# Low parts of the branch stage's weight slabs in pieces of 256 columns instead of 512

## The chip, the cores and the metric

The kernel runs on one core of one Trainium2 chip. The metric is the device time of one execution in microseconds, as the median of several runs; a profiled execution stands beside them.

## The reference

One layer of a transformer followed by the first layer of another, on 512 tokens of 1024 features, all in fp32:

```python
h = h + 0.5 * swiglu(rms_norm(h, ffn1_norm[i]), ...)          # up1, down1
u = rms_norm(h, mix_norm[i])
z = u @ w_in[i]                                               # the branch stage ("mix") begins
(aq, ak, av, iq, ik, iw, rq, rk, rv, rg, ga, gb) = jnp.split(z, split_points, axis=-1)
...
y_a = dsa_attention(aq, ak, av, iq, ik, iw, n_sel)            # top-k attention on roped aq, ak, iq, ik
y_r = group_norm_heads(retention(rq, rk, rv), ret_gn[i]) * jax.nn.silu(rg)
merged = jax.nn.sigmoid(ga) * (y_a @ w_branch_a[i]) + jax.nn.sigmoid(gb) * (y_r @ w_branch_b[i])
h = h + merged @ w_out[i]                                     # the branch stage ends
h = h + 0.5 * swiglu(rms_norm(h, ffn2_norm[i]), ...)          # up2, down2
gate = jax.nn.sigmoid(rms_norm(h, ple_norm[i]) @ w_ple_gate[i])
h = h + gate * (p[i] @ w_ple_proj[i])                         # ple
```

Then a gated linear attention mixer and a feed-forward block with a short convolution (gla, up3, down3), and a last norm. The stage that the change touches is the one from the product with `w_in` to the product with `w_out`.

## The kernel before

Activations lie feature-major: 8 chunks of 128 features by 512 tokens. A weight matrix is read as slabs of 128 partitions by up to 1024 columns (`SLAB = 8 * P`), one slab for each tile of 128 output features. Every product is made three times for fp32 accuracy: a weight and an activation are each split into a high part (`w_hi`, `u_hi`, in the rounded type fp32r) and a low part, the remainder (`w_lo`, `u_lo`). TensorE multiplies low by high, high by low and high by high into one accumulator (L1592 to L1594, 24 matmuls of 512 columns for a tile; L1782 to L1784 for the tiles of `rva`, with 328 columns).

A slab passes through a ring of `RING = 4` slots. SyncE loads it into `w_raw`; ScalarE copies it to `w_hi` in one instruction (L660, `hi_ready`); GpSimd subtracts, `w_lo = w_raw - w_hi` (`lo_part`, L574 to L579), and its last instruction counts up `lo_ready`. That semaphore tells TensorE that the slab can be used, and SyncE that the slot of `w_raw` can be loaded again. ScalarE may overwrite `w_hi` of a slot once TensorE has finished the tile that used it. So the low part of a slab is made some tiles ahead of its use.

The order of the branch stage is written out by hand in the list `MIX` (L76). Each engine walks through it and does its share of every step. A step such as `("rq", 0)` is a tile of a projection, `("to", k, ...)` stands for the part of a tile's contraction up to chunk k, between which small steps (index scores, retention scores, logits, attention) are placed. On GpSimd (L618 to L637) the loop before each step makes the low parts of the slabs up to four slots ahead of the step, then the step's own work: `rotate` for the ROPE steps (L608, L610, L612: a product with the cosine, one of the swapped halves with the sine, their sum, 512 columns each), the addition of the negative mean to `rv` (L629), and the low part of the retention output (L635). All of that stands in one queue, in the order of `MIX`.

Two accumulations of the program matter around it. The accumulator has `BANKS = 4` banks in PSUM, and tile t needs tile t - 4 to have been read out (`tile_freed`). The ROPE tiles are read out by VectorE (L1248) into one of two buffers of `gate_t`, so VectorE waits before the z-th of them until GpSimd has finished the rotation two before (`rope_ready`, L1246). The halves are swapped by DMAs that SyncE issues (L526), in one queue with the slab loads (L470) and the copies of the rotated keys (L530, L531), which wait for the first rotation.

The first steps of the stage, in the order of PSUM tiles: rg (head 0, half 0), kk, iq 0 to 3, rq 0, rk 0, rg (head 0, half 1), then the four tiles of `rva` (v of head 0, av and iw, token-major, one tile for 128 tokens). Their matmuls go chunk by chunk over all four tiles, so the four banks must be free within the first chunk:

```python
for c in range(first, upto):
    ...
    for tt in range(NT):
        if c == 0:
            free_bank(t + tt)
```

Of the kernel before, what the change touches and what calls it, by code (L numbers as in the profile page):

```python
# [45 lines left out]
RING = 4  # L46
# [3 lines left out]
SLAB = 8 * P  # L50
# [134 lines left out]
def layer_program(nc, A, out):  # L185
    plan = Plan()
# [11 lines left out]
    with ExitStack() as ctx:  # L198
# [221 lines left out]
        def nth(steps, step):  # L420
            return steps.index(step)
# [146 lines left out]
        @block.gpsimd  # L568
        def _(pool):
            pool.memset(ones[:, :], 1.0).then_inc(consts_set, 1)  # L570
            pool.memset(eps[:, 0:1], NORM_EPS).then_inc(consts_set, 1)
            pool.memset(eps[:, 1:2], GN_EPS).then_inc(consts_set, 1)

            def lo_part(slot, width, count):  # L574
                pool.wait_ge(hi_ready, count)
                for at in range(0, width, SLAB // 2):
                    part = slice(at, min(at + SLAB // 2, width))
                    ins = pool.tensor_tensor(w_lo[:, slot, part], w_raw[:, slot, part], w_hi[:, slot, part].bitcast(F32), ALU.subtract)  # L578
                ins.then_inc(lo_ready, 1)  # L579

            def lo_run(n0, n1):

                rounds = (n1 - n0) // RING
                if rounds:
                    with pool.Fori(0, rounds) as i:
                        for j in range(RING):
                            lo_part((n0 + j) % RING, SLAB, i * RING + (n0 + j + 1))
                for n in range(n0 + rounds * RING, n1):
                    lo_part(n % RING, SLAB, n + 1)

            def lo_down(n0):
                with pool.Fori(0, 2) as i:
                    for j in range(4 * DOWN_SLABS):
                        lo_part((n0 + j) % RING, plan.width[n0 + j], i * (4 * DOWN_SLABS) + (n0 + j + 1))

            def rotate(of):

                kind, z = of[0], nth(rope_steps, of)
                cos, sin = (cos_r[:, :], sin_r[:, :]) if kind in ("rq", "rk") else (cos_a, sin_a)
                dst = {"kk": lambda: wts[:, 0:S], "iq": lambda: q8[:, of[1], :], "aq": lambda: q8[:, of[1], :],  # L600
                       "rq": lambda: rqk[:, 0, :], "rk": lambda: rqk[:, 1, :]}[kind]()
                x, y = gate_t[:, z % 2, :], up_t[:, z % 2, :]
                pool.wait_ge(tile_freed, plan.first[of][1] + 1)
                if kind in ("rq", "rk") and of[1]:
                    pool.wait_ge(rs_done, NT * of[1])
                if kind == "aq":
                    pool.wait_ge(idx_scored, A_HEADS * len(index_units))
                pool.tensor_tensor(dst, x, cos, ALU.mult)  # L608
                pool.wait_ge(swapped[z % 2], 16 * sum(2 if s[0] in ("rq", "rk") else 4 for s in rope_steps[z % 2:z + 1:2]))
                pool.tensor_tensor(y, y, sin, ALU.mult).then_inc(rotated, 1)  # L610
                pool.wait_ge(rotated, z + 1)
                pool.tensor_tensor(dst, dst, y, ALU.add).then_inc(rope_ready, 1)  # L612

            def at(name):
                return plan.first[name][0]
            lo_run(0, at("down1"))
            lo_down(at("down1"))
            n = at("mix")  # L618
            for step in MIX:
                slabs = PROJECTS.get(step[0], (0, 0))[0]  # L620
                while n < plan.first[step][0] + slabs + RING and n < at("up2"):
                    lo_part(n % RING, plan.width[n], n + 1)
                    n += 1
                if step[0] in ("rv", "rva"):

                    for i in range(2):
                        pool.wait_ge(mean_ready, 2 * step[1] + i + 1)
                        part, mean = rv[:, step[1] % 2, 2 * i:2 * i + 2, :], v_mean[:, 4 * (step[1] % 2) + 2 * i:4 * (step[1] % 2) + 2 * i + 2]
                        pool.tensor_tensor(part, part, mean.unsqueeze(2).to_broadcast([P, 2, R_V]), ALU.add).then_inc(rv_ready, 1)  # L629
                if step[0] == "rlo":  # L630

                    for half in range(2):
                        pool.wait_ge(split_hi, nth(split_steps, (step, half)) + 1)
                        c = 2 * step[1] + half
                        pool.tensor_tensor(yr_lo[:, c, :], y_sq[:, half, :], yr_hi[:, c, :].bitcast(F32), ALU.subtract).then_inc(yr_ready, 1)  # L635
                if step[0] == "rot":
                    rotate(step[1:])  # L637
            lo_run(at("up2"), at("down2"))
            lo_down(at("down2"))
            lo_run(at("ple"), at("gla"))  # L640
            for n in range(at("gla"), at("gla") + 3):
                lo_part(n % RING, plan.width[n], n + 1)
            lo_run(at("gla") + 3, at("down3"))
            lo_down(at("down3"))
            pool.wait_ge(gained, len(POOL_OUT))
            pool.wait_ge(rstd_copied, 1)
            for c in POOL_OUT:
                pool.tensor_tensor(h[:, c, HALF:S], h[:, c, HALF:S], rstd[:, HALF:S], ALU.mult).then_inc(out_pool, 1)
# [1491 lines left out]
```

## Time and profile before

| | |
|---|---|
| median of 3 runs | 1864.43 us (1864.09 to 1866.12) |
| profiled execution | 1868.06 us, its span 1866.3 us |
| TensorE busy | 1838.2 us, 98% |
| VectorE, ScalarE, GpSimd busy | 784.6, 705.5, 906.9 us |
| GpSimd: low parts (L578) | 821.6 us in 634 instructions |
| granted TensorE clock | 0.996 of full speed |
| branch stage, first to last tile | about 372 to 848 us of the span |

The profile is of one execution. An engine's busy time is the union of its instructions; weight loads of TensorE lie beside its matmuls. A line of the timeline merges instructions of one kind that follow each other (x2, x8) and gives the idle time of the engine before them with what ended it. Consecutive matmuls overlap in it, so idle time of TensorE shows only where it exceeds the overlap.

### The profile page before, as it was taken

The numbers are of one execution on the slowest core, as the hardware profiler recorded it, in microseconds if no ns is written. First come the engines' busy times: TensorE is split into PE (matmuls) and PEld (weight loads), VectorE is DVE, ScalarE is ACT, GpSimd is POOL, SyncE is SP. The second block draws the span as 40 slices with busy tenths as digits, with TensorE's granted clock in tenths as the row PEclk, the third lists the DMA queues.
The fourth block names the chain that finished last, engine by engine and source line by source line (L and its number), as shares of the span: only waits on it lengthen the run. The fifth ranks groups of instructions, "written<-read, shape, count | busy, mean of one in ns | idle before, by whom it ended". The sixth has DMA issues, their size and how long they took to land.

```text
span 1866.3 us, 23858 instructions
## 1 busy us (share of the span) xinstructions
PE 1838.2 (98%) x8578; PEld 1494.8 (80%) x8578; DVE 784.6 (42%) x1295; ACT 705.5 (38%) x948; POOL 906.9 (49%) x710
## 2 busy tenths in 40 slices
PE   8999999999999999999999999999999999999998
PEld 6888888887778668888888888888877888888887
DVE  4222236225666654244222212256756374545312
ACT  6443422232233652244434422246344444444221
POOL 5444455386657424454444445353423455454542
PEclk9999999999999999999999999999999999999999
DMA  5323333243322212332232233232212222323331
GB/s 183 104 91 101 97 98 94 66 140 101 115 85 85 85 46 83 98 98 94 95 99 98 87 99 99 87 112 71 80 68 68 91 96 96 101 90 99 93 99 48
DMA packets 53556, 174.58 MB, mean 94 GB/s; under 512 B 6368, under 2 KB 8672, under 8 KB 53488
## 3 DMA queue, kind: packets, MB, share of 16 engines
q1 hardware_dynamic: 53312, 173.37, 29.1%
q8 instruction: 44, 0.72, 0.2%
q10 hardware_dynamic: 176, 0.30, 0.1%
q14 instruction: 24, 0.20, 0.0%
HBM read 166.56 MB, written 2.10 MB: 90 GB/s over the span
## 4 chain that ended last, share of the span: by engine, by line
PE 95%; DVE 2%; ACT 1%; issue 0%; DMA 0%; POOL 0%; POOLq 0%; DVEq 0%; ACTq 0%
PE acc L1592 28%; PE acc L1594 28%; PE acc L1593 28%; PE acc L1695 1%; PE acc L1697 1%; PE acc L1696 1%; PE aux L1847 1%; PE aux L1877 1%; PE acc L1999 0%; PE acc L1994 0%; PE acc L1898 0%; PE aux L1836 0%; PE aux L1985 0%; ACT w_hi L660 0%; PE aux L1829 0%
## 5 line engine op out<-in xcount | busy, mean ns | idle before, releaser
L578 POOL TENSOR_TENSOR w_lo<-w_raw,w_hi 128x512 fp32r<-128x512 f32 x634 | 821.6, 1319 | 924.4 <-ACT w_hi L660 924.4
L1592 PE MATMUL acc<-u_hi,w_lo 128*128 128x512 f32 x1560 | 618.5, 396 | 0.0
L1594 PE MATMUL acc<-u_hi,w_hi 128*128 128x512 f32 x1560 | 608.5, 390 | 0.0
L1593 PE MATMUL acc<-u_lo,w_hi 128*128 128x512 f32 x1560 | 608.3, 390 | 0.0
L660 ACT ACTIVATE w_hi<-w_raw 128x1024 fp32r<-128x1024 f32 (+1 forms) x317 | 326.3, 1034 | 543.2 <-PE acc L1594 460.5
L1592 PEld LDWEIGHTS acc<-u_hi,w_lo 128*128 128x128 f32 x1560 | 293.3, 188 | 72.3 <-issue 9.9
L1593 PEld LDWEIGHTS acc<-u_lo,w_hi 128*128 128x128 f32 x1560 | 293.4, 188 | 62.5 <-issue 2.9
L1594 PEld LDWEIGHTS acc<-u_hi,w_hi 128*128 128x128 f32 x1560 | 293.2, 188 | 61.4
L1592 PE MATMUL acc<-hid_hi,w_lo 128*128 128x512 f32 (+1 forms) x550 | 209.7, 381 | 0.0
L1593 PE MATMUL acc<-hid_lo,w_hi 128*128 128x512 f32 (+1 forms) x550 | 209.4, 381 | 0.0
L1594 PE MATMUL acc<-hid_hi,w_hi 128*128 128x512 f32 (+1 forms) x550 | 209.4, 381 | 0.0
L1592 PEld LDWEIGHTS acc<-hid_hi,w_lo 128*128 128x128 f32 x550 | 103.4, 188 | 19.9
L1593 PEld LDWEIGHTS acc<-hid_lo,w_hi 128*128 128x128 f32 x550 | 103.4, 188 | 19.7
L1594 PEld LDWEIGHTS acc<-hid_hi,w_hi 128*128 128x128 f32 x550 | 103.4, 188 | 19.6
L1061 DVE TENSOR_TENSOR tmp<-acc,rstd 128x512 f32<-128x512 f32 x44 | 30.4, 691 | 193.6 <-PE acc L1594 193.6
L1176 DVE SCALAR_TENSOR_TENSOR h<-acc,h 128x512 f32<-128x512 f32 x23 | 15.9, 692 | 220.5 <-PE acc L1594 220.5
L701 ACT ACTIVATE hid_hi<-tmp 128x512 f32 (+1 forms) x44 | 27.8, 632 | 199.9 <-DVE tmp L1064 199.9
L725 ACT ACTIVATE tmp<-tmp,cols 128x512 f32<-128x512 f32 x44 | 35.9, 816 | 117.3 <-DVE tmp L1083 117.3
L1083 DVE TENSOR_TENSOR tmp<-acc,rstd 128x512 f32<-128x512 f32 x44 | 30.3, 691 | 95.8 <-PE acc L1594 95.8
L1059 DVE TENSOR_TENSOR tmp<-acc,rstd 128x512 f32<-128x512 f32 x44 | 30.4, 691 | 91.8 <-PE acc L1594 91.4
L1695 PE MATMUL acc<-w_hi,u_lo 128*128 128x256 f32 x192 | 55.1, 287 | 0.0
L1697 PE MATMUL acc<-w_hi,u_hi 128*128 128x256 f32 x192 | 54.4, 283 | 0.0
(328 smaller groups left out, 2071.2 us busy)
## 6 DMA issues: line engine op xcount, KB each, us to landing
w_raw<-in_w_up SPq DMA_DIRECT2D x132, 512.0 KB, 3.5
w_raw<-in_w_mix SPq DMA_DIRECT2D x67, 512.0 KB, 3.8
w_raw<-in_w_down SPq DMA_DIRECT2D x48, 512.0 KB, 3.5
w_raw<-in_w_gla SPq DMA_DIRECT2D x30, 512.0 KB, 3.2
w_raw<-in_w_down SPq DMA_DIRECT2D x24, 384.0 KB, 3.1
w_raw<-in_w_ple SPq DMA_DIRECT2D x10, 512.0 KB, 3.7
tmp<-tmp SPq DMA_DIRECT2D x36, 64.0 KB, 2.0
h<-in_xT SPq DMA_DIRECT2D x8, 256.0 KB, 5.2
```

What stands on the lines that cost most here:

```text
L578: ins = pool.tensor_tensor(w_lo[:, slot, part], w_raw[:, slot, part], w_hi[:, slot, part].bitcast(F32), ALU.subtract)
L660: act.activation(w_hi[:, slot, 0:width], w_raw[:, slot, 0:width], ACT.Copy).then_inc(hi_ready, 1)
L701: act.activation(hid_hi[:, i2 + b, :], up_t[:, b, :], ACT.Copy).then_inc(prod_hi, 1)
L725: act.activation(dst, (z_gate, z_up)[part][:, 2:2 + S], ACT.Identity, scale=conv_col("conv_w2", i2, p, part), bias=conv_col("conv_b", i2, ...
L1059: dve.tensor_tensor(gate_t[:, b, :], acc[:, (t0 + 2 * b) % BANKS, :], rstd[:, :], ALU.mult).then_inc(tile_freed, 1)
L1061: dve.tensor_tensor(up_t[:, b, :], acc[:, (t0 + 2 * b + 1) % BANKS, :], rstd[:, :], ALU.mult).then_inc(tile_freed, 1)
L1083: dve.tensor_tensor((z_gate, z_up)[part][:, 2:2 + S], acc[:, (t0 + c) % BANKS, :], rstd[:, :], ALU.mult).then_inc(tile_freed, 1)
L1592: pe.matmul(o, w_lo[:, slot, columns], x_hi, start=first, stop=False)
L1593: pe.matmul(o, w_hi[:, slot, columns], x_lo, start=False, stop=False)
L1594: return pe.matmul(o, w_hi[:, slot, columns], x_hi, start=False, stop=last)
L1695: pe.matmul(o, u_lo[:, k, blk(tt)], w_hi[:, slot, columns], start=k == 0, stop=False)
L1697: last = pe.matmul(o, u_hi[:, k, blk(tt)], w_hi[:, slot, columns], start=False, stop=k == KD - 1)
```

## The change

`lo_part` gets a parameter for the width of a piece, and the branch stage's loop passes a quarter of a slab, 256 columns; everywhere else it stays half a slab, 512. The wait for `hi_ready` stands before the first piece and `lo_ready` is counted up by the last, as before.

```diff
-            def lo_part(slot, width, count):
+            def lo_part(slot, width, count, size=SLAB // 2):
                 pool.wait_ge(hi_ready, count)
-                for at in range(0, width, SLAB // 2):
-                    part = slice(at, min(at + SLAB // 2, width))
+                for at in range(0, width, size):
+                    part = slice(at, min(at + size, width))
                     ins = pool.tensor_tensor(w_lo[:, slot, part], w_raw[:, slot, part], w_hi[:, slot, part].bitcast(F32), ALU.subtract)
                 ins.then_inc(lo_ready, 1)
...
                 while n < plan.first[step][0] + slabs + RING and n < at("up2"):
-                    lo_part(n % RING, plan.width[n], n + 1)
+                    lo_part(n % RING, plan.width[n], n + 1, SLAB // 4)
                     n += 1
```

On GpSimd, from the slab behind the rotation of kk to the one behind the rotation of iq 1, the program before (w_raw, w_hi and w_lo are the ring; q, tmp and side belong to the rotations of iq 0 and iq 1):

```order
L578 TENSOR_TENSOR w_lo<-w_raw,w_hi 128x512 x2
L608 TENSOR_TENSOR q<-tmp,side 128x512
L610 TENSOR_TENSOR tmp<-tmp,side 128x512
L612 TENSOR_TENSOR q<-q,tmp 128x512
L578 TENSOR_TENSOR w_lo<-w_raw,w_hi 128x512 x4
L608 TENSOR_TENSOR q<-tmp,side 128x512
L610 TENSOR_TENSOR tmp<-tmp,side 128x512
L612 TENSOR_TENSOR q<-q,tmp 128x512
L578 TENSOR_TENSOR w_lo<-w_raw,w_hi 128x512
L578 TENSOR_TENSOR w_lo<-w_raw,w_hi 128x472
```

and the program after:

```order
L578 TENSOR_TENSOR w_lo<-w_raw,w_hi 128x256 x4
L608 TENSOR_TENSOR q<-tmp,side 128x512
L610 TENSOR_TENSOR tmp<-tmp,side 128x512
L612 TENSOR_TENSOR q<-q,tmp 128x512
L578 TENSOR_TENSOR w_lo<-w_raw,w_hi 128x256 x8
L608 TENSOR_TENSOR q<-tmp,side 128x512
L610 TENSOR_TENSOR tmp<-tmp,side 128x512
L612 TENSOR_TENSOR q<-q,tmp 128x512
L578 TENSOR_TENSOR w_lo<-w_raw,w_hi 128x256 x3
L578 TENSOR_TENSOR w_lo<-w_raw,w_hi 128x216
```

Nothing moved past anything else: each slab's subtraction is in twice as many pieces, and the three instructions of a rotation keep their 512 columns. TensorE, VectorE and ScalarE have the same instructions in the same order in both programs.

## Rows read from the trace of the kernel before

**Rows 1.** The page, section 4: the chain that ended last, by engine.
```profile
PE 95%; DVE 2%; ACT 1%; issue 0%; DMA 0%; POOL 0%; POOLq 0%; DVEq 0%; ACTq 0%
```

**Rows 2.** Windows: stretch, us, busy us of each engine, clock, DMA share, GB/s.
```profile
385.00:440.00 55.00, 55.00 (x276) 47.77 (x275) 10.48 (x25) 11.69 (x13) 47.03 (x40) 1.00 0.47 135
...
600.00:720.00 120.00, 112.94 (x527) 77.60 (x526) 69.31 (x194) 61.36 (x122) 50.40 (x39) 1.00 0.21 69
...
sum 475.00, PE 464.51 PEld 362.19 DVE 237.45 ACT 173.14 POOL 266.67; mean PE 92.90 PEld 72.44 DVE 47.49 ACT 34.63 POOL 53.33
```

**Rows 3.** Groups by line and form on GpSimd: form, count, busy us, mean ns, idle before.
```profile
L578 POOL TENSOR_TENSOR w_lo<-w_raw,w_hi 128x512 fp32r<-128x512 f32 x604 | 800.4, 1347 | 924.4 <-ACT w_hi L660 924.4
L578 POOL TENSOR_TENSOR w_lo<-w_raw,w_hi 128x256 fp32r<-128x256 f32 x24 | 17.7, 737 | 0.0
```

**Rows 4.** Timeline of GpSimd: start, us, instruction, count, [idle before it <-releaser].
```profile
375.02 10.03 POOL L578 TENSOR_TENSOR w_lo<-w_raw,w_hi 128x512 fp32r<-128x512 f32 x8 [13.77 <-ACT w_hi L660]
388.10 2.54 POOL L578 TENSOR_TENSOR w_lo<-w_raw,w_hi 128x512 fp32r<-128x512 f32 x2 [3.05 <-ACT w_hi L660]
...
394.47 2.55 POOL L578 TENSOR_TENSOR w_lo<-w_raw,w_hi 128x512 fp32r<-128x512 f32 x2
...
400.99 1.29 POOL L610 TENSOR_TENSOR tmp<-tmp,side 128x512 f32<-128x512 f32 x1 [2.72 <-DMA tmp<-tmp]
...
403.60 5.04 POOL L578 TENSOR_TENSOR w_lo<-w_raw,w_hi 128x512 fp32r<-128x512 f32 x4
...
412.47 2.46 POOL L578 TENSOR_TENSOR w_lo<-w_raw,w_hi 128x512 fp32r<-128x512 f32 x2
...
421.36 1.29 POOL L612 TENSOR_TENSOR q<-q,tmp 128x512 f32<-128x512 f32 x1
```

**Rows 5.** Timeline of SyncE's queue, 375 to 450 us.
```profile
394.54 0.51 SPq L530 DMA_DIRECT2D ikd<-wts  x1
...
397.01 2.49 SPq L526 DMA_DIRECT2D tmp<-tmp  x4
```

**Rows 6.** Timeline of VectorE, 375 to 450 us.
```profile
422.75 0.69 DVE L1248 TENSOR_TENSOR tmp<-acc,rstd 128x512 f32<-128x512 f32 x1 [3.18 <-POOL q L612]
423.36 0.68 DVE L1243 TENSOR_TENSOR srg<-acc,rstd 128x512 f32<-128x512 f32 x1
```

**Rows 7.** Timeline of TensorE, near 378 and 424 us.
```profile
378.07 0.49 PE L1592 MATMUL acc<-u_hi,w_lo 128*128 128x512 f32 x1
...
424.09 0.42 PE L1782 MATMUL acc<-w_hi,u_lo 128*128 128x328 f32 x1
```

**Rows 8.** Line 1288 on VectorE, 385 to 860 us: count, ns min/median/max.
```profile
L1288 DVE TENSOR_TENSOR ssum<-y_sq x4: 681/1236/1674, 466.1 to 610.3; 128x512 f32<-128x512 f32 x4
```

**Rows 9.** Timeline of VectorE and of TensorE, near 611 us.
```profile
610.30 1.67 DVE L1288 TENSOR_TENSOR ssum<-y_sq 128x512 f32<-128x512 f32 x1
...
612.03 0.72 PE L1857 MATMUL aux<-ones,ssum 128*128 128x1 f32 x5 [0.74 <-DVE ssum L1288]
```

**Rows 10.** Timeline of GpSimd, before 611 us.
```profile
593.61 2.53 POOL L578 TENSOR_TENSOR w_lo<-w_raw,w_hi 128x512 fp32r<-128x512 f32 x2 [1.70 <-ACT w_hi L660]
...
610.14 1.29 POOL L578 TENSOR_TENSOR w_lo<-w_raw,w_hi 128x512 fp32r<-128x512 f32 x1
```

**Rows 11.** Line 1330 (ns min/median/max), then timeline of VectorE and TensorE, near 640.
```profile
L1330 DVE TENSOR_SCALAR probs<-probs,small x8: 478/480/1514, 636.3 to 640.1; 128x512 f32<-128x512 f32 x8
...
636.30 5.32 DVE L1330 TENSOR_SCALAR probs<-probs,small 128x512 f32<-128x512 f32 x8
...
641.68 0.44 PE L1887 MATMUL aux<-consts,probs 128*128 128x128 f32 x2 [0.78 <-DVE probs L1330]
```

**Rows 12.** Timeline of VectorE, GpSimd and TensorE, 449 to 460 us.
```profile
450.02 5.99 DVE L1261 SCALAR_TENSOR_TENSOR bias<-tmp,avt,bias 128x512 f32<-128x512 f32 x6 [1.11 <-ACT tmp L841]
...
449.92 1.26 POOL L578 TENSOR_TENSOR w_lo<-w_raw,w_hi 128x512 fp32r<-128x512 f32 x1
...
459.82 0.60 PE L1847 MATMUL aux<-wts,rv 128*128 128x128 f32 x3 [0.48 <-DVE wts L1281]
```

## The prediction, made before the changed kernel ran

> **What bounds the kernel now.** I read the chain that ended last first: 95% of it is TensorE and nothing of it is GpSimd [rows 1]. So GpSimd time counts only where a TensorE wait hangs on it. Next the windows over the branch stage (385 to 860 us). TensorE is idle there for 475.00 - 464.51 = 10.49 us in all: none in 385 to 440, 7.06 us in 600 to 720 [rows 2]. That is the whole purse out of which shorter waits can be paid, 0.6% of the run, and most of those waits end on ScalarE or VectorE work that the change does not touch. The granted clock is 1.00 in each of these windows, so matmul time itself is not at stake. GpSimd is busy 266.67 of the 475 us, but 47.03 of 55 us in the first window [rows 2]: there it is nearly full, elsewhere it idles for ScalarE's high part.
>
> **What the change adds on GpSimd.** Of the 70 slabs of the stage, 67 have 1024 columns (2 instructions before, 4 after), two have 984 (2 to 4), one 656 (2 to 3): 140 become 279, 139 more. The columns stay the same, so what is added is the fixed part of an instruction. A 512-column one takes 1.29 us where nothing disturbs it [rows 10] and eight in a row take 10.03 us, 1.25 from start to start [rows 4]: neighbours overlap by 0.04. A 256-column one, from the narrow slabs of the other stages, has a mean of 0.737 [rows 3], so 0.70 from start to start. Two halves are 1.39 against 1.25: 0.14 to 0.15 us more for each instruction added, and I take 0.145. The bounds are 0 (time in proportion to columns) and 2 x 0.737 - 1.29 = 0.18. That is 139 x 0.145 = 20 us more busy GpSimd, nearly all under TensorE. The Trainium skill (GPSIMD Engine Reference, section 3.1, "Elementwise — side-by-side cycle accounting") gives about 2.6 cycles an element at 1.2 GHz for two inputs, and 4497 ns for 2048 columns. As an estimate from that page a column costs 2.17 ns and an instruction only some 60 ns besides; by it the loss below would be 8 x 0.06 = 0.5 us instead of 1.16, and the sum would end 0.7 us lower. The two forms in [rows 3] speak for the larger fixed part.
>
> **Where this reaches TensorE: the rotations before rva.** The third and later ROPE tiles are read out of PSUM by VectorE (L1248) only when an earlier rotation on GpSimd is done; that for rk 0 starts at 422.75, 0.1 us after the rotation of iq 3 ends (421.36 + 1.29 = 422.65), and the copy of rg behind it at 423.36 [rows 4, 6]. These two free the accumulator banks of the third and fourth rva tile, the latter at 423.36 + 0.69 = 424.05. TensorE starts the fourth at 424.09, with a first matmul of 0.42 us, long for 328 columns [rows 7]: it runs 0.04 us behind GpSimd although no idle time shows. Back from there: GpSimd is without a gap from 400.99, when the swapped halves of iq 0 land. They are issued by SyncE at 397.01, behind the copies of the keys that wait for the rotation of kk until 394.54 [rows 5]. That rotation runs without a gap from the slab at 388.10 [rows 4]. The slabs on this chain are the one at 388.10 (2 more instructions), the two at 403.60 (4 more) and the one at 412.47 (512 and 472 columns become 256, 256, 256 and 216: 2 more). The slab at 394.47 is off it, since 2.72 us of idle time before 400.99 hide its 0.29. So 8 x 0.145 = 1.16 us, and TensorE loses **1.16 us** (0 to 1.44 by the bounds). The start at 388.10 hangs on VectorE copies near 385 that dodge GpSimd pieces; I let that move it by 0.3 either way. Nothing gives the loss back, as the next steps follow TensorE.
>
> **What the change takes away: VectorE's waits for GpSimd.** VectorE instructions that read two SBUF tensors, and some copies and scalings, stand still until the GpSimd instruction that is running ends. At 610.30 the sum of the two squares begins, GpSimd's subtraction has begun at 610.14 and ends at 611.43; the sum takes 1.67 us, against 0.68 undisturbed, and TensorE is idle 0.74 us for it [rows 8 to 10]. A piece of half the length ends such a wait sooner. I go through the three places where a wait of this kind ends an idle time of TensorE.
> - 612.03: from 593.61 GpSimd runs without a gap [rows 10] and carries 2 slabs, 4 more instructions, 0.58 us. The instruction under way when VectorE arrives is then the rotation's last, ending at 611.43 - 1.29 + 0.04 + 0.58 = 610.76 instead of 611.43 [rows 10]. Gain 0.67 of the 0.74 idle [rows 9].
> - 641.68: eight scalings of probs take 5.32 us; the last two meet the two pieces of a slab, and the longest takes 1.51 where the middle one takes 0.48; TensorE is idle 0.78 for them [rows 11]. With pieces of 0.74 each of the two waits about half as long, 1.0 us less in all. Gain 0.78, all that is idle.
> - 450 to 460: six weighted sums take 5.99 us where 0.85 each, as they follow each other undisturbed, would be 5.1 [rows 12]; the first waits until 451.18, when the instruction of 449.92 ends. This VectorE chain feeds the idle times of TensorE up to 459.82, the last 0.48. Half-length pieces release the first up to 0.9 earlier, but four instead of two are in the queue and GpSimd, later by 0.87, meets the next three sums as well, at some 0.15 each. Gain 0.5, bounds -0.4 and 0.96.
> Against this stands a new wait of about 0.1 us at 809, where VectorE's last mg subtraction is late by a hair now and would meet the second of two pieces. Gain 0.67 + 0.78 + 0.5 - 0.1 = **1.85 us**.
>
> **Where a late low part could bite and does not.** With RING = 4 a slab's low part is made three or more tiles (5.4 us each) ahead. The tightest is the second slab of the stage: GpSimd begins at 375.02, is done 2.55 us later, and TensorE needs it at 378.07 [rows 4, 7]. 0.29 us fits into this 0.5.
>
> **The sum.** The profiled execution took 1868.06 us (span 1866.3): 1868.06 + 1.16 - 1.85 = 1867.4. It stands 3.6 us over the median of the runs shown, and the difference carries over: 1864.43 - 0.7 = **1863.7 us**. Bounds of the terms: +1.44 + 0.3 with no gain but the -0.4 of the third place gives +2.2; the opposite corner, no fixed part and all waits taken off, gives -2.8.
>
> **Rivals.**
> - Only the loss. VectorE's arrivals fall differently on the pieces and the gains of three places cancel; the mixed stretch of many short VectorE steps speaks for that. 1864.43 + 1.2 = 1865.6.
> - Mostly gain. The waits halve everywhere, the clash at 450 is light, and the rva tiles lose under 0.5 us. 1864.43 - 2.2 = 1862.2. The trace has but 10.49 us of idle TensorE in the stage, so a gain over 3.7 us would need a third of that, far more than the three places hold. This is also where the page's smaller fixed part points: 1863.0, by the Trainium skill's GPSIMD Engine Reference.
> - Slower, outright: GpSimd fills up in 385 to 440. There it has 7.97 us left, and 21 instructions are added. At 0.145 they take 3.0 us and the engine stays under 51 of 55. It decides from 0.38 us apiece, when nothing is left; at 0.47, 8 x 0.47 = 3.8 us go straight to the rva tiles, 1868.2. The 256-column row (0.737 whole) speaks against it; for it speaks only that VectorE, let in at twice as many boundaries, may hold GpSimd up each time, and VectorE is busy just 10.48 us there.
> - That the change moves something else: the listing shows TensorE, VectorE and ScalarE with the same instructions in the same order, so no.
>
> **How the numbers follow.** A measurement of this kernel can tell about 0.2% (3.7 us) from no change. Forecast 0.6, only the loss 0.2, mostly gain 0.12: all three within 0.2%. Slower by more 0.05, and faster by more 0.03. The range takes the first three with their bounds, +2.2 and -2.8, and what runs of one kernel differ by (1864.09 to 1866.12): 1861.5 to 1866.9. Faster 0.03, same 0.92, slower 0.05.
>
> **What would show it.** In the changed trace: 256-column subtractions of 0.74 us, GpSimd busy 20 us more; a new wait of TensorE of about 1.1 us at the fourth rva tile near 424; the sum of squares near 611 down from 1.67 to about 1.2 and the idle time before it nearly gone; the last two scalings near 640 at about 1 us each. Wrong would be: low parts named as what TensorE waits for, no wait at 424, or a 256-column piece of over 0.9 us.

## The result: 0.44% slower, two instructions held

The changed kernel took 1872.69 us (median of 6 runs, 1872.22 to 1877.18) where the kernel before took 1865.99 beside it (6 runs, 1864.09 to 1867.26): ratio 1.0044, 95% interval 1.0034 to 1.0054. The medians differ by 6.7 us; the ratio is estimated from all the runs, two of the changed kernel's at 1877 among them, and comes to 8.2 us. The forecast was 1863.7 with a range up to 1866.9, so the time lies outside it, and on the side that had a chance of 0.05. The profiled execution took 1872.3 us (span 1870.5, before 1866.3).

First the page: busy time of each engine, share and instructions, then the chain that ended last by engine. Under it the stretches of the branch stage (us, busy us and instructions of each engine, granted clock, DMA share, GB/s).

```profile
PE 1837.1 (98%) x8578; PEld 1493.7 (80%) x8578; DVE 780.0 (42%) x1295; ACT 705.1 (38%) x948; POOL 929.0 (50%) x849
...
PE 92%; DVE 3%; ACT 2%; POOL 2%; issue 1%; DMA 0%; SPq 0%; POOLq 0%; DVEq 0%; ACTq 0%
```
```profile
385.00:440.00 55.00, 52.94 (x258) 46.14 (x257) 7.86 (x13) 9.15 (x10) 48.30 (x53) 0.97 0.47 135
440.00:520.00 80.00, 74.05 (x352) 54.54 (x351) 58.41 (x107) 24.36 (x35) 49.36 (x59) 0.98 0.28 86
...
600.00:720.00 120.00, 113.58 (x531) 78.03 (x530) 64.36 (x191) 62.44 (x123) 56.96 (x67) 1.00 0.21 66
...
sum 475.00, PE 459.73 PEld 358.80 DVE 230.13 ACT 168.56 POOL 284.07; mean PE 91.95 PEld 71.76 DVE 46.03 ACT 33.71 POOL 56.81
```

The second stretch in the kernel before:

```profile
440.00:520.00 80.00, 77.42 (x372) 57.27 (x371) 57.26 (x110) 26.36 (x38) 50.25 (x40) 1.00 0.27 86
```

Against [rows 1, 2] and this row: TensorE is idle 475.00 - 459.73 = 15.27 us of the stage, not 10.49, and the new idle time lies in the first two stretches (2.06 us instead of none, 5.95 instead of 2.58). In the same two the granted clock is no longer 1.00. In the list of what TensorE waits for, two entries over 1 us are new: L1829 for the wts of L1281 on VectorE, once, 4.7 us, and L1782 for the tmp of L1248, once, 2.1 us.

Each goes back to one instruction of VectorE. The timelines of VectorE and of GpSimd about the first (start, us, instruction, count, [idle before it <-releaser]); this execution runs 0.51 us ahead of the one before from its start-up (374.51 against 375.02 in [rows 4]). The kernel before comes last:

```profile
383.57 2.36 DVE L1200 COPY cos_r<-tmp 128x512 f32<-128x512 f32 x1
...
424.46 0.69 DVE L1248 TENSOR_TENSOR tmp<-acc,rstd 128x512 f32<-128x512 f32 x1 [3.14 <-POOL q L612]
```
```profile
374.51 11.14 POOL L578 TENSOR_TENSOR w_lo<-w_raw,w_hi 128x256 fp32r<-128x256 f32 x16 [13.00 <-ACT w_hi L660]
388.69 0.74 POOL L578 TENSOR_TENSOR w_lo<-w_raw,w_hi 128x256 fp32r<-128x256 f32 x1 [3.04 <-ACT w_hi L660]
```
```profile
384.08 1.26 DVE L1200 COPY cos_r<-tmp 128x512 f32<-128x512 f32 x1
```

The copy L1200 (0.43 us where nothing disturbs it) starts at 383.57, under the piece of GpSimd that began at 383.52 and ended at 384.27. It is not let in there. Two more pieces pass, GpSimd's stream ends at 374.51 + 11.14 = 385.65, and only then does the copy get through. Before, it took 1.26 us at 384.08 and waited for one piece. But that piece was the eighth and last of its stream ([rows 4]: 375.02 + 10.03 = 385.05), so this row doesn't tell a wait for the piece from a wait for the stream. The second, about the multiplication L1258, again with the kernel before last:

```profile
448.33 6.91 DVE L1258 TENSOR_SCALAR bias<-tmp,avt 128x512 f32<-128x512 f32 x1 [1.46 <-ACT tmp L841]
455.36 0.75 DVE L1261 SCALAR_TENSOR_TENSOR bias<-tmp,avt,bias 128x512 f32<-128x512 f32 x1
456.03 1.15 DVE L1281 TENSOR_TENSOR wts<-aux,dec 128x512 f32<-128x512 f32 x2
```
```profile
441.88 8.36 POOL L578 TENSOR_TENSOR w_lo<-w_raw,w_hi 128x256 fp32r<-128x256 f32 x12 [2.56 <-ACT w_hi L660]
450.19 2.05 POOL L629 TENSOR_TENSOR rv<-rv,small 128x512 f32<-128x512 f32 x2
452.18 2.78 POOL L578 TENSOR_TENSOR w_lo<-w_raw,w_hi 128x256 fp32r<-128x256 f32 x4
```
```profile
438.61 7.50 POOL L578 TENSOR_TENSOR w_lo<-w_raw,w_hi 128x512 fp32r<-128x512 f32 x6 [1.65 <-ACT w_hi L660]
...
445.06 1.34 DVE L1258 TENSOR_SCALAR bias<-tmp,avt 128x512 f32<-128x512 f32 x1 [1.46 <-ACT tmp L841]
```

6.91 us for work of 0.43. It stands under the tenth piece of a stream, and GpSimd runs the rest of that piece, two further pieces, two additions of 512 columns and four more pieces past it, until its queue is empty at 454.96. Before, L1258 took 1.34 us at 445.06: it arrived under the sixth piece and was let in at that piece's end, with two additions and two pieces still to come. TensorE's side of the two, and the stretches around them:

```profile
425.21 0.42 PE L1782 MATMUL acc<-w_hi,u_lo 128*128 128x328 f32 x1 [2.06 <-DVE tmp L1248]
...
457.32 1.22 PE L1829 MATMUL aux<-ikd,q 64*128 64x512 f32 x2 [4.68 <-DVE wts L1281]
```
```profile
424.00:426.00 2.00, 0.79 (x4) 0.65 (x5) 1.29 (x2) 0.00 (x0) 2.00 (x4) 1.00 0.61 234
426.00:430.00 4.00, 4.00 (x17) 4.00 (x17) 0.00 (x0) 1.58 (x2) 3.92 (x5) 0.57 0.80 214
430.00:434.00 4.00, 4.00 (x29) 4.00 (x28) 0.00 (x0) 0.00 (x0) 4.00 (x6) 1.00 0.43 134
...
456.00:460.00 4.00, 2.68 (x6) 1.27 (x8) 2.59 (x5) 1.19 (x3) 0.00 (x0) 0.60 0.02 4
```

Just behind the first idle time and at the end of the second the granted clock falls to 1.2 GHz, each time for some 3.4 us: 17 multiplications fit into 426 to 430 where 29 fit into the next 4 us. By the rows the first fall costs (1 - 0.57) x 4 = 1.7 us, the second up to 1.6. So the stage holds 15.27 - 10.49 = 4.8 us more idle time and at most 3.3 us of slower clock, 8 us in all. The spans differ by only 4.2 us because the profiled execution of the kernel before lost clock elsewhere, in the last mixer, where the changed one did not:

```profile
1270.00:1282.00 12.00, 11.84 (x83) 11.65 (x83) 7.65 (x20) 3.19 (x6) 3.41 (x2) 0.86 0.17 48
1290.00:1300.00 10.00, 10.00 (x31) 6.52 (x30) 5.12 (x9) 8.54 (x12) 3.21 (x3) 0.83 0.40 137
```

That is the kernel before; 0.14 x 12 + 0.17 x 10 = 3.4 us. With the changed kernel the same part (1270 to 1310) is at 1.00.

The gains came as well. Line 1288, to be set against [rows 8], and line 1330, against [rows 11]:

```profile
L1288 DVE TENSOR_TENSOR ssum<-y_sq x4: 682/892/1031, 473.4 to 617.7; 128x512 f32<-128x512 f32 x4
```
```profile
L1330 DVE TENSOR_SCALAR probs<-probs,small x8: 481/482/966, 643.2 to 646.4; 128x512 f32<-128x512 f32 x8
```

The waits of 0.7 us (L1857) and 0.8 us (L1887 for VectorE) are gone from the list of TensorE's waits. Part of the second comes back at once: the next group of L1887 now waits 0.82 us for ScalarE, where it waited 0.25.

### The profile page after: what moved, and what is told of

It is laid out like the page before. It is cut to its first block, busy times and chain, and to the rows that moved or that the text cites. A ratio compares the mean times of both kernels' runs of the same rounds, so it can differ in the third digit from the quotient of the medians.

```text
span 1870.5 us, 23997 instructions
## 1 busy us (share of the span) xinstructions
PE 1837.1 (98%) x8578; PEld 1493.7 (80%) x8578; DVE 780.0 (42%) x1295; ACT 705.1 (38%) x948; POOL 929.0 (50%) x849
## 4 chain that ended last, share of the span: by engine, by line
PE 92%; DVE 3%; ACT 2%; POOL 2%; issue 1%; DMA 0%; SPq 0%; POOLq 0%; DVEq 0%; ACTq 0%
PE acc L1592 27%; PE acc L1594 27%; PE acc L1593 27%; PE acc L1695 1%; PE acc L1696 1%; PE acc L1697 1%; PE aux L1847 1%; POOL w_lo L578 1%; PE aux L1877 1%; PE acc L1999 0%; PE acc L1994 0%; ACT w_hi L660 0%; PE acc L1898 0%; PE aux L1829 0%; DVE bias L1258 0%
## 5 line engine op out<-in xcount | busy, mean ns | idle before, releaser
L578 POOL TENSOR_TENSOR w_lo<-w_raw,w_hi 128x512 fp32r<-128x512 f32 (+3 forms) x773 | 844.6, 1119 | 907.6 <-ACT w_hi L660 907.5
L1696 PE MATMUL acc<-w_lo,u_hi 128*128 128x256 f32 x192 | 54.3, 283 | 0.0
```

Source lines behind the costliest of these rows:

```text
L1696: pe.matmul(o, u_hi[:, k, blk(tt)], w_lo[:, slot, columns], start=False, stop=False)
```

## The experiments

The question after the two traces: is the whole loss in the two held instructions, and what holds them? Seven kernels change only which slabs of the stage have short pieces, or, in whole, make each slab one piece; two more, two_input and fill, change another engine's work and are given at their place. The size in the call of `lo_part` (`at("mix")` is the number of the stage's first slab):

```
lo_part(n % RING, plan.width[n], n + 1, SIZE)   # after: SIZE = SLAB // 4 in all of the stage
late:   SLAB // 2 if n < at("mix") + 17 else SLAB // 4
early:  SLAB // 4 if n < at("mix") + 13 else SLAB // 2
mid:    SLAB // 4 if at("mix") + 13 <= n < at("mix") + 17 else SLAB // 2
ahead:  SLAB // 4 if at("mix") + 13 <= n < at("mix") + 15 else SLAB // 2
behind: SLAB // 4 if at("mix") + 15 <= n < at("mix") + 17 else SLAB // 2
free:   SLAB // 2 if n - at("mix") in (0, 1, 2, 3, 13, 14) else SLAB // 4
whole:  SLAB
```

**Which part loses: late, early, mid.**

> The first 17 slabs of the branch stage (up to the retention output of head 0) keep pieces of 512 columns, the other 53 have 256. Theory A (all the loss sits in two places, 424 and 448 us, and both are gone): no idle time over 1 us before 500, the waits at 612 and 641 shortened as in the changed kernel (0.7 and 0.9 us, of which half comes back as a wait for ScalarE); 0.5 to 1.5 us below the kernel before. Theory C (the 139 added instructions cost a little everywhere): 53 of 70 slabs still carry them, so some 5 us above the kernel before.

> Only the first 13 slabs of the branch stage have pieces of 256 columns, all later ones 512. Theory A: the rva tiles start 2.1 us late near 424, and the clock falls for 3.4 us behind it (1.7 us more); VectorE's scaling at L1258 near 448 meets pieces of 512 and waits for one of them, at most 1.3 us; the kernel is 3.5 to 4.5 us above the one before. Rival B (L1258 stands still for 6.9 us because GpSimd is late, whatever its pieces are): both waits come, 7 to 9 us above.

> Only slabs 14 to 17 of the branch stage (GpSimd at 438 to 451 us) have pieces of 256 columns, the others 512. Theory A: no wait near 424; L1258 cannot get in between the short pieces and takes 4 us or more, TensorE is idle over 2 us near 450, and the clock may fall behind it; 3 to 6 us above the kernel before. Rival B: L1258 takes at most 1.3 us and the kernel is within 1 us of the one before. Rival D (it depends on the moment at which L1258 arrives): either, with the time in the trace telling which.

Measured against the kernel before: late 1.0002 (0.9992 to 1.0011), early 1.0024 (1.0015 to 1.0034), mid 1.0020 (1.0010 to 1.0031). So 53 of the 70 slabs in short pieces, all of the late ones, change nothing that can be measured (the gain of 0.5 to 1.5 us that was expected of late isn't seen either). The loss of early and the loss of mid add up to the 0.44% of the whole change. The four slabs of mid alone, 8 instructions more, lose 0.2%. The rows, for early and for mid, L1200 and L1258 on VectorE:

```profile
L1200 DVE COPY cos_r<-tmp x1: 2357/2357/2357, 383.5 to 383.5; 128x512 f32<-128x512 f32 x1
...
L1258 DVE TENSOR_SCALAR bias<-tmp,avt x1: 1341/1341/1341, 448.3 to 448.3; 128x512 f32<-128x512 f32 x1
```
```profile
L1200 DVE COPY cos_r<-tmp x1: 1260/1260/1260, 383.1 to 383.1; 128x512 f32<-128x512 f32 x1
...
L1258 DVE TENSOR_SCALAR bias<-tmp,avt x1: 6921/6921/6921, 444.1 to 444.1; 128x512 f32<-128x512 f32 x1
```

Each hold comes with the short pieces around it and without the other; early has the wait of 2.06 us at 425.19, mid the one of 4.69 at 453.08, late neither. Mid's profiled execution has half clock for twice as long beside its wait as the changed kernel's, (0.47 + 0.38) x 4 = 3.4 us lost:

```profile
452.00:456.00 4.00, 2.92 (x8) 1.27 (x8) 2.56 (x5) 1.40 (x3) 0.00 (x0) 0.53 0.00 0
456.00:460.00 4.00, 4.00 (x14) 2.62 (x12) 3.49 (x7) 1.44 (x3) 0.00 (x0) 0.62 0.03 6
```

**Is it the kind of VectorE instruction: two_input.** In the changed kernel the multiplication by a column becomes one of two tensors:

```
-dve.tensor_scalar(score, sq[:, j % 2, 0:nk], w, None, ALU.mult).then_inc(idx_added, 1)
+dve.tensor_tensor(score, sq[:, j % 2, 0:nk], w.to_broadcast([P, nk]), ALU.mult).then_inc(idx_added, 1)
```

> The changed kernel with one thing altered: the scaling at L1258 (one SBUF tensor and a scalar for each partition) is written as a product of two SBUF tensors, the second one a broadcast column. Theory A (it is the form of the VectorE instruction that is kept out; forms with two SBUF inputs get in after the running piece): the instruction takes 0.7 to 1.3 us, the idle 4.7 us near 452 and the clock fall behind it go, and the kernel is 1.5 to 3 us above the one before instead of 7. Rival E (any instruction that contends with GpSimd would have waited): unchanged, 7 us above.

Measured: 1872.8 us, 1.0043 (1.0027 to 1.0060), and the instruction is held all the same.

```profile
448.80 7.19 DVE L1258 TENSOR_TENSOR bias<-tmp,avt 128x512 f32<-128x512 f32 x1 [1.46 <-ACT tmp L841]
```

The theory that only the copy and scaling forms are passed over is out. On the two forms the Trainium skill (SBUF — State Buffer, "Who interferes with whom") says that copies and scalings can take the pair of ports that VectorE shares with GpSimd, that an instruction with two SBUF inputs contends for its read side, and that the pair is an exclusive lock that whoever issues first has for one whole instruction. Both forms do contend here, and before the change L1258 waited to the end of the running piece (1.34 us). What the page doesn't tell is who has the lock next when GpSimd's pieces follow each other; that an instruction is passed over by two further instructions (2.36 us) or by eight (6.91 us) goes beyond its rule, and the trace decides.

**What lies before the arrival or what lies after it: ahead, behind.** Mid's stream has 12 short pieces, and L1258 arrives under the tenth. One kernel keeps the short pieces ahead of the arrival, one those behind.

> Of the four slabs that the slow run had in short pieces (the kernel called mid), the first two are back at 512 columns, the last two have 256. The multiplication L1258 arrives at about 444 us in the second or third short piece, after two slabs of long ones. Runway of short pieces: too few short pieces ran before it, so it is let in after one, 1.3 us or less, TensorE's idle time near 453 us stays at about 0.5 us, time 1865 to 1867. Short pieces ahead of it alone decide: held until the queue empties, near 6.9 us as in mid, 1870 to 1871.

> The other two of the four slabs: the first two have 256 columns, the last two 512. L1258 arrives at about 444 us under a piece of 512 columns, with eight short ones behind it and only long ones ahead. Runway of short pieces: held for more than one piece, up to the end of the stream (5 us or more), time 1869 to 1871. Short pieces ahead of it alone decide: let in after one piece, 1.3 to 1.7 us, time 1865 to 1867.

GpSimd's stream and L1258, first ahead, then behind:

```profile
437.49 8.07 POOL L578 TENSOR_TENSOR w_lo<-w_raw,w_hi 128x256 fp32r<-128x256 f32 x10 [1.62 <-ACT w_hi L660]
...
443.94 6.35 DVE L1258 TENSOR_SCALAR bias<-tmp,avt 128x512 f32<-128x512 f32 x1 [1.47 <-ACT tmp L841]
```
```profile
437.67 7.97 POOL L578 TENSOR_TENSOR w_lo<-w_raw,w_hi 128x512 fp32r<-128x512 f32 x8 [1.60 <-ACT w_hi L660]
...
444.12 0.94 DVE L1258 TENSOR_SCALAR bias<-tmp,avt 128x512 f32<-128x512 f32 x1 [1.46 <-ACT tmp L841]
```

(The group's form is that of its first piece; ahead is eight pieces of 256 and two of 512, behind four of 512 and four of 256.) Both arrive 6.45 us behind the start of the stream. In ahead, eight pieces have finished, a piece of 512 columns is running, only long ones follow, and L1258 is held 6.35 us: 1.0025 (1.0015 to 1.0034). In behind six have finished, short ones are running and following, and it is let in at the end of the running one: 1.0004 (0.9994 to 1.0014). So not the width at the arrival or after it holds VectorE; the past does, and it looks like a count.

**The count by itself: micro, sweep, sweep2, sweep3.** Four stand-alone programs. GpSimd runs a stream of the same subtraction; a chosen piece raises a semaphore, and on it VectorE runs one copy of 128x512 (in the first three by way of a short instruction on ScalarE). From sweep:

```
for i in range(lead + AHEAD):          # AHEAD: 10 in sweep and sweep2, 8 in sweep3
    ...
    ins = pool.tensor_tensor(w_lo[:, to], w_raw[:, part], w_hi[:, part].bitcast(F32), ALU.subtract)
    if i == lead - 1:
        ins.then_inc(begun, 1)
```

> A stand-alone program that leaves out the whole computation of the reference; its time as a whole means nothing. GpSimd runs streams of the same subtraction in pieces of 128, 256, 512 or 1024 columns, and VectorE starts one instruction of 512 columns (a copy, or a multiplication by a column) at eight instants inside one piece, in one half of the trials after a short run of undisturbed pieces (1 to 3), in the other after a long one (about 6 us: 15, 8, 5 or 3 pieces); 8 to 14 us of stream (4 to 13 pieces) are still ahead then. Runway theory (an instruction of VectorE finds no gap once GpSimd has run undisturbed for long with short pieces): 256 after the short run at most 0.43 + 0.73 us, that is under 1.3 us each; 256 after the long run 3 us or more in most trials, up to the rest of the stream; 512 and 1024 under 0.43 + one piece (1.7 and 2.9 us) after either. Piece-length theory (short pieces shut VectorE out whenever they stand in a row): 256 and 128 are held several us after either run. Arrival-phase theory (what decides is the instant within the piece): of the eight instants some are held several us and some not, in the same way after the short run and after the long one.

Eight arrivals each (ns min/median/max). In order: 15 to 17 pieces of 128 columns before the copy; 8 or 9 of 256; 5 of 512. (2 or 3 of 256 are like the second.)

```profile
L69 DVE COPY c<-a x8: 4825/5105/5385, 107.8 to 193.6; 128x512 f32<-128x512 f32 x8
...
L71 DVE COPY c<-a x8: 456/757/1058, 311.5 to 405.8; 128x512 f32<-128x512 f32 x8
...
L73 DVE COPY c<-a x8: 676/954/1233, 539.8 to 645.9; 128x512 f32<-128x512 f32 x8
```

The instant within the piece only moves the wait within one piece's length, so that theory is out. But the runway theory as written missed too: after eight or nine pieces of 256 columns the copy was let in, every time. Held were only the arrivals behind fifteen pieces or more. That called for one step at a time:

> A second stand-alone program that leaves out the whole computation: one copy of 128x512 on VectorE (0.43 us undisturbed) arrives in a stream of GpSimd's subtractions after 1 to 20 pieces have run undisturbed, always with 9 to 10 pieces still to come; pieces of 128, 256 and 512 columns, once with no wait in the stream and once with a wait, already satisfied, before each 1024 columns as in the kernel. Count theory (what decides is how many instructions GpSimd has run without a pause; held in the kernel at 8, 9 and 13, let in at 7 or fewer, in the first program let in at 8 and held at 15): the same threshold between 8 and 15 for all three widths, from which the copy takes the rest of the stream, about 3.5, 6.5 and 12 us, also with 512 columns. Time theory (about 6 us of undisturbed stream): held from 16 pieces of 128, from 9 of 256 and from 5 of 512 columns. Short-piece theory: 512 columns are let in after one piece (1.7 us or less) at any count, 128 and 256 are held from a threshold of their own.

Twenty arrivals each, pieces of 128, 256 and 512 columns:

```profile
L67 DVE COPY c<-a x20: 426/427/4126, 6.0 to 179.5; 128x512 f32<-128x512 f32 x20
...
L69 DVE COPY c<-a x20: 694/697/6818, 363.1 to 643.4; 128x512 f32<-128x512 f32 x20
...
L71 DVE COPY c<-a x20: 1233/1234/12216, 940.5 to 1436.2; 128x512 f32<-128x512 f32 x20
```

In each series the first 14 arrivals take the short time and the last 6 the long one, with nothing between. The step, with 256 columns: behind 14 finished pieces, then behind 15.

```profile
527.77 0.69 DVE L69 COPY c<-a 128x512 f32<-128x512 f32 x1 [9.91 <-ACT pad L43]
...
545.20 6.82 DVE L69 COPY c<-a 128x512 f32<-128x512 f32 x1 [10.59 <-ACT pad L43]
```

The step lies at the same piece for all three widths, so it is a count of instructions: not a time (15 pieces take 6 to 18 us) and not a matter of short ones. With 512 columns the copy takes 12.2 us. In the kernel before only 5 pieces had finished when L1258 arrived, and L1200 came behind 7, under the last piece, with nothing left that could have passed it. The change made that 9 and 13, with pieces still to come.

> A third stand-alone program that leaves out the whole computation. Pieces of 256 columns only, 5 to 20 of them before the copy arrives, and six kinds of trial: base (as before), psum (VectorE also runs six multiplications of 8 columns out of PSUM at the start of the stream), copy (it also runs one copy of 512 columns there), tiny (one multiplication of 2 columns there), signal (each piece raises a semaphore), pause (six pieces, then an idle time of about 0.9 us of GpSimd, then the stream). In the second program the copy was held from 15 finished pieces on. Common-count theory (the pieces and VectorE's own instructions since GpSimd last paused are counted together, and 16 hold; in the kernel 17 or more were held and 15 or fewer let in): psum is held from about 9 finished pieces, tiny from 14, base, signal and pause from 15, copy from 15 or 16 after the copy, since an instruction that was let in starts the count again, or from 14 if it does not. Pieces-only theory: psum and tiny from 15 like base. If the pause does not start the count again: pause from 9.

Base, psum, tiny, signal and pause all step at 15, so VectorE's own short instructions do not count, and an idle time of GpSimd (1.2 us in pause) starts the count again; a full copy let in under the second piece moves the step to 17, that is, it starts the count again as well. The common-count theory is out. But 15 is not the kernel's number: L1258 was held behind 8 and 9 finished pieces and let in behind 5 and 6, and L1200 was held behind 13. L1288 was let in behind 13 instructions before the change and behind 16 after it. Other VectorE instructions stood between there, and GpSimd itself had idled for 0.08 us in front of the last sum of a rotation (before: from 607.50 + 1.30 to 608.88), one instruction or less before each arrival. If so short a pause starts the count again, L1288 is no exception; in sweep 0.2 us between two streams was enough, and 0.08 was not tested.

> A fourth stand-alone program that leaves out the whole computation. Pieces of 256 columns, 4 to 16 of them finished before the copy, 8 in all behind that; ten kinds of trial, each with one thing added that the kernel has beside the stream: six activations of ScalarE, four DMAs into SBUF, twelve multiplications of TensorE, three reductions on VectorE out of SBUF, four multiplications of 256 columns or two of 512 out of PSUM on VectorE, slabs (ScalarE writes each 1024 columns anew and GpSimd waits for it, as in the kernel), rv (the six instructions that VectorE has between 437 and 442 us in the kernel), and all of them but TensorE's. Base is held from 15 finished pieces on. If what stands beside the stream makes the kernel's instruction stay out from 8 finished pieces on, the kind that has it is held from well under 15 (rv and all from 9 or so if it is VectorE's own instructions; slabs and all if it is the wait at each slab; dma or scalar or matmul if it is those engines). If nothing beside the stream matters: 15 in all ten kinds, and the count in the kernel must begin before the pause at 436 us.

Measured: the step lies at 14 in base, at 13 beside activations or DMAs, at 15 beside TensorE's work, reductions or the four reads of PSUM, at 14 with the two reads of PSUM, with rv and with real waits at each slab, at 15 with all. Nothing that was added brings it down to 8, and base itself moved from 15 to 14 in this program, whose arrivals come earlier in the piece and whose tail is shorter. What lowers the count in the kernel stays open.

**The clock: fill.** Nine multiplications into a bank that is not in use, before the tile that waits at 424:

```
+if c == 0 and tt == 2:
+    claim(3)
+    for _ in range(9):
+        pe.matmul(aux[:, 3, :], w_hi[:, slot, 0:P], u_hi[:, 0, :], start=True, stop=True)
```

> The changed kernel with nine multiplications of 512 columns added before the tile at 424 us that waits for VectorE: they write a bank that is not in use and their result is not read, so TensorE has work in the 2.1 us in which it stood idle. If the idle time makes the granted clock fall (1.2 GHz for 3.4 us, 1.7 us of loss): no fall near 426 us, granted clock 1.00 there, TensorE's program after it 1.7 us earlier against the changed kernel from 430 us on; the time 1870.5 to 1871.5 with the fall at 457 us left, ratio to the kernel before 1.0025 to 1.0035. If the fall has another cause: clock 0.57 at 426 to 430 us as in the changed kernel and 1872 to 1873 us. In either case L1258 is held, as long as its arrival still falls under the stream.

```profile
426.00:430.00 4.00, 4.00 (x29) 4.00 (x28) 0.00 (x0) 1.58 (x2) 3.92 (x5) 1.00 0.88 272
```

The fall is gone: clock 1.00 and 29 multiplications where the changed kernel had 0.57 and 17. L1258 starts at 446.63, not at 448.33, 1.70 us earlier (0.2 of it from the start-up). So the idle time before it brought the clock down. The time as a whole, 1872.09 us, ratio 1.0033 (1.0021 to 1.0046), is above the 1870.5 to 1871.5 that were expected, 0.6 below the changed kernel's, and the intervals overlap: that the 1.5 us reach the end is not shown by it.

**The mirror: whole.** One instruction for each slab.

> The change mirrored: each subtraction of the branch stage has 1024 columns instead of 512, so a slab is one instruction. Count theory: at most 6 instructions of GpSimd stand in a row before any arrival, so VectorE is never held past the piece that is running: L1200 and L1258 take 0.43 us plus what is left of one piece, at most 2.9 us each; GpSimd is busy about 0.145 us less for each of 69 slabs, 10 us in all; the wait at 612 us may grow by 1.2 us and the one at 641 us by 1 us, the start of the tile at 424 us may come 0.6 us earlier; the time 1864.5 to 1868. If any long run of GpSimd holds VectorE: L1258 takes over 5 us and the time is 1870 or more.

No hold: L1200 took 0.66 us and L1258 0.92. Yet the time is 1871.8, ratio 1.0034 (1.0018 to 1.0049), above what was expected. Three of TensorE's waits in the stage, longer than before (0.5 and 0.7 us) or new, and two stretches:

```profile
PE aux L1829 <- DVE srg L1290: 1.6, 1, 1.6
PE aux L1857 <- DVE ssum L1288: 1.5, 1, 1.5
...
PE acc L1592 <- DVE mg_lo L1185: 0.9, 1, 0.9
```
```profile
610.00:618.00 8.00, 6.46 (x26) 5.04 (x25) 5.47 (x11) 1.84 (x3) 5.95 (x4) 0.79 0.68 225
626.00:632.00 6.00, 5.53 (x16) 2.52 (x17) 3.87 (x12) 2.28 (x3) 2.68 (x3) 0.72 0.25 87
```

Waits to the end of one piece of up to 2.4 us now cost at 467, 612 and 813: TensorE is idle 13.1 us of the stage instead of 10.5. The clock falls twice, (1 - 0.79) x 8 + (1 - 0.72) x 6 = 3.4 us. The two together are 6.0 us, against 6.3 by the medians. Long pieces lose by a wait for one piece, short ones by the count.

**The change without its two holds: free.**

> The changed kernel, but with 512 columns in six of the slabs: the first four, in whose stream L1200 arrives, and the two ahead of L1258. All else has 256, the slabs of the rotation chain among them. Theory (the loss is the two held instructions and what follows them, nothing else of the change): L1200 and L1258 take 1.5 us or less each, TensorE stands idle about 1.0 us before L1782 at 425 us (the 1.16 us of the prediction), the granted clock stays at 1.00 there, the gains at 612 and 641 us (0.6 and 0.8 us) come, and the time is 1864.5 to 1867, ratio 0.9995 to 1.001. If short pieces cost elsewhere too: 1868 or more, with a further idle time of TensorE over 1 us in the stage.

```profile
L1200 DVE COPY cos_r<-tmp x1: 817/817/817, 384.0 to 384.0; 128x512 f32<-128x512 f32 x1
...
L1258 DVE TENSOR_SCALAR bias<-tmp,avt x1: 934/934/934, 446.2 to 446.2; 128x512 f32<-128x512 f32 x1
```
```profile
374.91 10.48 POOL L578 TENSOR_TENSOR w_lo<-w_raw,w_hi 128x512 fp32r<-128x512 f32 x10 [13.76 <-ACT w_hi L660]
```
```profile
424.60 0.41 PE L1782 MATMUL acc<-w_hi,u_lo 128*128 128x328 f32 x1 [1.04 <-DVE tmp L1248]
```

1866.25 us, 1.0004 (0.9995 to 1.0014): with six slabs of long pieces and all the rest short, the loss of 0.44% is gone. This is the cause shown from the other side. It also speaks for a count inside the kernel. The stream of L1200 is six long and four short pieces here; the copy arrives 383.97 - 374.91 = 9.06 us behind its start, as in the changed kernel (383.57 - 374.51), but behind 8 finished pieces and not 13, and it is let in at the end of the ninth, with one still to come. So the time since the start doesn't decide there either. L1258 was held behind 8 (ahead), so the two don't share one exact number. Free is also the pure test of the sum: the wait at 425 is 1.04 us. No version beat the kernel before by what can be measured.

## Why the prediction was wrong, step by step

- **What bounds the kernel**: right as to where a loss could enter. "Matmul time itself is not at stake" was wrong. The granted clock was read as a constant of the stage, though it was 0.86 and 0.83 in two stretches of the last mixer in the same trace. It fell at both new idle times, which cost up to 3.3 us, a term that the prediction put at nothing. Fill shows the link for the first.
- **What is added on GpSimd**: right. 139 more instructions, 929.0 - 906.9 = 22.1 us more busy against 20. Sixteen pieces in 11.14 us are (11.14 - 0.74) / 15 = 0.69 from start to start, so 2 x 0.69 - 1.25 = 0.14 for each one added. The smaller fixed part of 60 ns, an estimate from the Trainium skill's GPSIMD Engine Reference, section 3.1, did not hold.
- **The chain to the rva tiles, 8 x 0.145 = 1.16**: right in size, though the wait shows before the third tile and not the fourth. The rotation chain ends 424.46 - 422.75 + 0.51 = 2.22 us late, of which the late start is 388.69 - 388.10 + 0.51 = 1.10, and 1.12 is left for the eight. Free has 1.04.
- **The start of the chain, "0.3 either way"**: the first step that failed, with 1.10. The copies were seen, their arrival under a stream of 16 short pieces too; what was taken for granted is that VectorE gets in when the running piece ends. No wait in the trace of before spoke against it, but the two that looked strongest could not test it: L1200 met the last piece of its stream, and L1288 at 610.30, where the prediction has GpSimd without a gap from 593.61, came 13 instructions behind that start but only one behind a gap of 0.08 us. No experiment stood behind the assumption.
- **The third place, 450 to 460, gain 0.5 (bounds -0.4 to 0.96)**: the second step that failed, by the same assumption. L1258, ahead of the six sums, was held 5.57 us longer than before, TensorE idle 4.68 us for it. The bounds let only the phase of an arrival vary, and never the rule. This and its clock fall are about half of the loss and the first hold with its own the other half: mid, which has the second alone, has the ratio 1.0020, early, which has the first, 1.0024. (By medians mid loses 5.3 us and early 4.3; mid's profiled execution has more half clock than the changed kernel's.)
- **612 and 641**: right. L1288 down from 1.67 to 1.03 and 0.74 us of idle time gone (0.67 forecast); the 0.78 at 641 gone, but 0.82 - 0.25 = 0.57 of it came back as a wait for ScalarE a microsecond later, which was not asked for: what is late next.
- **Late low parts, things moved**: right, none. The new wait of 0.1 us at 809 didn't come either.
- **The rival on the slow side** had the right sign and one of the two places for the wrong reason. Its 21 added instructions in 385 to 440 take in the stream that begins at 438.61 and runs past that stretch; the changed trace has 32 subtractions there instead of 19, 13 more, and GpSimd is busy 48.30 us instead of 47.03. It asked whether VectorE, let in at twice as many boundaries, would hold GpSimd up. VectorE wasn't let in at all. Doubling a count had been priced as time only.

## What to carry to other kernels

When GpSimd's work is cut into shorter instructions, count what stands in a row before each contending instruction of VectorE as well as adding up the time: behind a long uninterrupted row VectorE waits for the end of the stream, not of the piece. A pause of GpSimd, a VectorE instruction let in early, or longer pieces just there keep the count low, and one late instruction on the path to TensorE can cost more than the fixed parts that were added ahead of it (4.7 us of idle TensorE for L1258, 1.1 us for the eight instructions of the rotation chain). And a granted clock of 1.00 in the trace of before is no promise for a kernel in which TensorE gets a new idle time: the one of 2.06 us lost 1.7 us more to half clock.

## What the chip did that was not expected

- Behind 15 finished GpSimd instructions a VectorE copy takes 4.1, 6.8 or 12.2 us with ten pieces of 128, 256 or 512 columns from its arrival to the end of the stream, behind 14 it takes 0.43, 0.70 or 1.23. The first held arrival was behind 13 to 15 in the stand-alone programs; for L1258 in the kernel it lies at 7 or 8, for L1200 somewhere in 9 to 13. Why it differs is open.
- With the idle times of TensorE of 2.06 us (at 425) and 4.68 us (at 457) went 1.2 GHz for 3.4 us each, with the 4.69 us of mid for 6.8 us; the 1.04 us in free at 424.6 had none. In whole a fall came behind an idle time of 1.54 us, and another behind one of 1.75, which the kernel before has too (it ends at 624.55) without a fall. So these runs show no length that decides.
